# Summing, normalising and scattering tokens inside the expert loop of a mixture-of-experts decoder step

## What is computed

```python
def _moe(x, w_router, router_bias, w_gate, w_up, w_down):
    scores = jax.nn.sigmoid(h @ w_router)
    biased = scores + router_bias
    grp_top = lax.top_k(biased.reshape(T, 4, 4), 2)[0]      # 4 groups of 4 experts
    group = jnp.argmax(grp_top.sum(-1), axis=-1)            # best group
    ...                                                     # top 2 experts inside it
    wts = wts / wts.sum(-1, keepdims=True)
    for e in range(N_EXPERTS):
        he = jax.nn.silu(h @ w_gate[e]) * (h @ w_up[e])
        y = y + gates[:, e:e + 1] * (he @ w_down[e])

x = LN(alpha * x + moe(x))                                  # alpha = 4 ** 0.25
```

## Time and profile before

| | us |
|---|---|
| median of 3 runs (1121.09 to 1126.28) | 1123.17 |
| span of the profiled execution | 1120.2 |
| TensorE busy | 1026.5 (92%) |
| VectorE busy | 497.7 (44%) |
| ScalarE busy | 330.4 (29%) |
| GpSimd busy | 116.9 (10%) |

### The profile page before, as it was taken

The page is one execution under the profiler, slowest core; times in us unless marked ns, Lnnn a source line. Parts: engine busy times, 40 slices in busy tenths (PEclk is TensorE's granted clock), DMA queues, the critical chain, the costliest instruction groups (busy, mean ns, idle before and its releaser), DMA issues.

```text
span 1120.2 us, 25522 instructions
## 1 busy us (share of the span) xinstructions
PE 1026.5 (92%) x10346; PEld 676.0 (60%) x10346; DVE 497.7 (44%) x1257; ACT 330.4 (29%) x877; POOL 116.9 (10%) x140
## 2 busy tenths in 40 slices
PE   9999997599998499999899999989999948999995
PEld 3687454466664267777788887656555535666641
DVE  1581134322222636497636653866623252222217
ACT  0102114133333233223334332165422132333321
POOL 0010000210000300000211110421000011100013
PEclk9999998699999699999999999899999978999998
DMA  9762204999996631122322233394353089999936
GB/s 317 298 88 65 109 38 194 334 351 373 371 402 251 218 151 60 54 86 75 95 75 77 73 115 99 110 388 183 127 222 150 19 324 285 375 372 378 413 105 222
DMA packets 80861, 225.32 MB, mean 201 GB/s; under 512 B 9424, under 2 KB 50432, under 8 KB 62432
## 3 DMA queue, kind: packets, MB, share of 16 engines
q1 hardware_dynamic: 65184, 153.29, 37.7%
q0 software_dynamic: 11968, 57.71, 15.6%
q10 hardware_dynamic: 3584, 12.58, 3.0%
HBM read 201.57 MB, written 40.86 MB: 216 GB/s over the span
## 4 chain that ended last, share of the span: by engine, by line
PE 86%; DMA 5%; DVE 4%; issue 4%; ACT 1%; POOL 0%; DVEq 0%; POOLq 0%; SPq 0%; ACTq 0%
PE bank L1352 16%; PE bank L1256 10%; PE bank L1543 9%; PE bank L1376 8%; PE bank L1451 6%; PE bank L1642 4%; PE bank L1477 3%; PE bank L1334 2%; PE bank L1514 2%; DMA xkept<-x 1%; PE bank L1896 1%; PE bank L1921 1%; PE bank L1267 1%; DMA work<-xkept,idx 1%; PE bank L1855 1%
## 5 line engine op out<-in xcount | busy, mean ns | idle before, releaser
L1256 PE MATMUL bank<-ring,cat 128*128 128x512 f32 x256 | 112.6, 594 | 1.3 <-ACT cat L2088 1.3
L1543 PE MATMUL bank<-xT,ring 128*128 128x288 f32 x448 | 110.9, 407 | 0.0
L1543 PEld LDWEIGHTS bank<-xT,ring 128*128 128x128 f32 x448 | 84.6, 190 | 23.8 <-issue 1.1
L1352 PE MATMUL bank<-ring,work 128*32 128x128 f32 (+1 forms) x1344 | 82.4, 317 | 1.7 <-DVE work L2537 1.7
L1256 PEld LDWEIGHTS bank<-ring,cat 128*128 128x128 f32 x256 | 47.5, 190 | 57.2 <-issue 57.2
L2547 DVE TENSOR_TENSOR work<-work,bank 128x192 f32<-128x192 f32 x32 | 11.3, 354 | 156.3 <-ACT work L2048 156.3
L2556 DVE COPY work<-bank 64x512 f32<-64x512 f32 x64 | 44.0, 688 | 67.2 <-PE bank L1376 66.7
L1352 PEld LDWEIGHTS bank<-ring,work 128*32 128x32 f32 (+1 forms) x1344 | 57.8, 121 | 24.7 <-issue 12.7
L1451 PE MATMUL bank<-xT,ring 128*128 128x288 f32 x256 | 63.1, 407 | 0.0
L2048 ACT ACTIVATE work<-bank 128x192 f32<-128x192 f32 x32 | 10.6, 331 | 162.3 <-PE bank L1352 162.3
L1451 PEld LDWEIGHTS bank<-xT,ring 128*128 128x128 f32 x256 | 48.3, 190 | 13.5 <-issue 0.4
(11 more groups left out here) (459 smaller groups left out, 1893.8 us busy)
## 6 DMA issues: line engine op xcount, KB each, us to landing
ring<-in_stream_dram SPq DMA_DIRECT2D x61, 1024.0 KB, 9.9
work<-in_stream_dram SPq DMA_DIRECT2D x16, 1024.0 KB, 17.1
cat<-in_stream_dram SPq DMA_DIRECT2D x16, 1024.0 KB, 19.1
by_batch<-in_pages_dram SPq DMA_DIRECT2D x128, 128.0 KB, 2.4
x<-in_stream_dram SPq DMA_DIRECT2D x12, 1024.0 KB, 18.3
xT<-in_stream_dram SPq DMA_DIRECT2D x12, 1024.0 KB, 17.3
yrows<-work ACTq DMA_DIRECT2D x32, 384.0 KB, 7.4
lnp<-in_ln_dram POOLq DMA_DIRECT2D x4, 1024.0 KB, 15.2
```

Of the source, the lines that this page charges most:

```text
L1256: i = pe.matmul(bank(n)[0:ROWS[tile], :], cat[:, k, tok(tile)], slot(w[k // 4], 4, 512)[:, k % 4, :], start=(k == 0), stop=(k == KC - 1))
L1352: i = pe.matmul(by_half[rows * q:rows * q + rows, :, to:to + width], xgT[:, e % 2, k, at:at + rows], w[:, :, width * q:width * q + width], ...
L1543: i = pe.matmul(bank(n + s)[:, 0:nn], slot(w, KC, 256)[:, k, P * (m % 2):P * (m % 2) + P], xT[:, k, a:a + nn], start=(k == 0), stop=(k == ...
```

## The change

The gathers of outputs after the loop are gone. Each token is completed in a slot of the later of its two experts:

- The experts are worked in a new order, `ORDER`: 0, 4, 8, 12, 1, 5, ... Position j holds group j % 4, so the two experts of a token are a multiple of four positions apart. The columns of the router follow it, and `route` indexes them so.
- For each slot three things are found in the head of the stage (`weigh_slots` on VectorE, `slot_lists` on TensorE, a copy on ScalarE): the gate divided by alpha, the row of `part_row` if this expert is the token's first, and the row of `final_row` if it is the second. A row number past the end means that the indirect DMA is to leave the slot out (`bounds_check`, `oob_is_err=False`).
- For the expert e - 2, in iteration e: ScalarE copies the wide part of the output; VectorE adds gate times output to the gathered rows (`add_part`). GpSimd scatters the sum of first experts to `parts` in DRAM (`keep_part`, positions 0 to 11), and before the sum of a second expert it fetches these rows over the gathered ones (`fetch_part`, positions 4 to 15). Each of these waits until the scatter of the position before has landed.
- For positions 4 to 15 VectorE averages, centres and applies scale and shift; ScalarE sums the squares; GpSimd takes the power -1/2 (`invert`) and scatters the finished rows (`write_final`) to `xnext` in layer 0 and to the output in layer 1. All 96 slots are computed; only the rows whose second expert this is are written.
- Gathers have six buffers instead of four. GpSimd issues gather(e+3) in iteration e, after fetch_part(e+1) and before keep_part(e-2).
- In layer 0 SP waits for all final scatters and loads the five tiles of x from `xnext`; TensorE then turns them. The ten gathers, the sums by TensorE, the stores by ScalarE and the stores by SP at the end are gone. `parts` is filled once with x from the input by a DRAM to DRAM copy on SP's queue in layer 0's output projection.

Its core:

```diff
+ORDER = [EPG * (j % NG) + j // NG for j in range(N_EXP)]
-NXG = 4
+NXG = 6
+EARLY_ROWS = 4
@@ gpsimd
+                def part_landed(e):
+                    pool.wait_ge(part_kept[layer], 16 * (e + 1))
+
+                def keep_part(e):
+                    if e > 0:
+                        part_landed(e - 1)
+                    elif layer == 0:
+                        pool.wait_ge(parts_cleared, 16)
+                    pool.wait_ge(summed, (N_EXP - 1) * layer + e + 1)
+                    pool.indirect_dma_start(
+                        out=parts, out_offset=bass.IndirectOffsetOnAxis(ap=part_row[0:CAP, e:e + 1], axis=0),
+                        in_=xg[e % NXG][0:CAP, :], in_offset=None,
+                        bounds_check=T - 1, oob_is_err=False).then_inc(part_kept[layer], 16)
+
+                def fetch_part(e):
+                    take(pool, ejob(layer, e, "T1"))
+                    part_landed(e - NG)
+                    if e > NG:
+                        pool.wait_ge(part_back[layer], 16 * (e - NG))
+                    pool.indirect_dma_start(out=xg[e % NXG][0:CAP, :], in_=parts, ... final_row[0:CAP, e:e + 1] ...)
+
+                def invert(e):
+                    pool.wait_ge(squared_rows, final_count(layer, e))
+                    pool.tensor_scalar(row_rstd[...], row_var[...], LN_EPS / ALPHA ** 2, None, ALU.add).then_inc(widened, 1)
+                    pool.wait_ge(widened, final_count(layer, e))
+                    pool.tensor_tensor(row_rstd[...], row_rstd[...], c("minus_half", CAP), ALU.pow).then_inc(inverted_rows, 1)
+
+                def write_final(e):
+                    pool.wait_ge(finished, final_count(layer, e))
+                    if e - NZB >= NG:
+                        pool.wait_ge(rows_final[layer][e % NZB], 16 * ((e - NG) // NZB))
+                    pool.indirect_dma_start(out=xnext if layer < LAYERS - 1 else outs["x"], ... final_row[0:CAP, e:e + 1] ...)
+
+                    for e in range(EARLY_ROWS, NXG):
+                        take(pool, ejob(layer, e - EARLY_ROWS, "T1"))
+                        gather_rows(e)
+                    ln_params(2 * layer + 1)
+                    pool.wait_ge(slots_weighed, layer + 1)
+                    for e in range(2, N_EXP + 2):
+                        if NG <= e + 1 < N_EXP:
+                            fetch_part(e + 1)
+                        if NXG <= e + 3 < N_EXP:
+                            part_landed(e + 3 - NXG)
+                            if e + 3 - NXG >= NG:
+                                pool.wait_ge(finished, final_count(layer, e + 3 - NXG))
+                            gather_rows(e + 3)
+                        if e - 2 < N_EXP - NG:
+                            keep_part(e - 2)
+                        if NG <= e - 2:
+                            invert(e - 2)
+                            write_final(e - 2)
+                    landed_finals(pool, layer)
@@ tensor, ahead of the loop
+                slot_lists()
                 turn_rows(0)
@@ vector, the loop
+                    now(dve.memset(row_sum, 0.0))
+                    weigh_slots(layer)
+                    for e in range(-1, N_EXP):
                         if e + 1 < N_EXP and e != 0:
                             copy_rows(e + 1)
-                        if e < 0:
-                            weigh(layer)
-                        if 0 <= e < N_EXP:
+                        if e >= 2:
+                            add_part(e - 2)
+                        if e - 2 >= NG:
+                            average(e - 2)
+                            center_rows(e - 2)
+                        if e >= 0:
                             n = ejob(layer, e, "GU")
                             ...
+                        if e - 2 >= NG:
+                            affine_rows(e - 2)
+                    add_part(last - 1)
+                    average(last - 1)
+                    add_part(last)
+                    average(last)
+                    for e in (last - 1, last):
+                        center_rows(e)
+                        affine_rows(e)
@@ scalar, the loop, between the copy of the turned result and Silu
+                        if 2 <= e <= N_EXP:
+                            copy_wide(e - 2)
+                        if NG <= e - 2:
+                            square(e - 2)
@@ sync, after the loop
+                        landed_finals(sp, layer)
+                        if layer < LAYERS - 1:
+                            for tile in range(NT):
+                                sp.dma_start(x[0:ROWS[tile], tile, :], xnext[tok(tile), :]).then_inc(tile_loaded[tile], 16)
```

More of the change, by code:

```diff
@@ L82, in constant_table @@
     put("ones", np.ones((P, P)))
-    put("rowbase", np.tile(CAP * np.arange(N_EXP) - 1.0, (P, 1)))
-    put("token", i + P * np.arange(NT)[None, :] * 1.0)
+    put("minus_half", np.full((P, 1), -0.5))
+    put("token", i + P * np.arange(NT)[None, :] - 1.0 * NO_ROW)
     put("lneps", np.full((P, 1), LN_EPS))
@@ L1078, in pool_mixture @@
                     pool.dma_start(xkept[tok(tile), :], x[0:ROWS[tile], tile, :]).then_inc(x_kept, 16)
-                landed(pool, job(f"{layer}.list0"), 1)
+                pool.wait_ge(idx_named, layer + 1)
                 pool.wait_ge(x_kept, 16 * NT * (layer + 1))
-                for e in range(NXG):
+                for e in range(EARLY_ROWS):
                     gather_rows(e)
@@ L2338, in affine @@
                 step(dve.reciprocal(rstd[0:r, one], rstd[0:r, one]))
-                for half, ready in enumerate((ln_left, last)):
+                for half, ready in enumerate((ln_left, ln_done)):
                     cols = slice(512 * half, 512 * half + 512)
```

476 lines of the change are left out of this document (236 added, 240 removed).

## The result

The changed kernel takes 1185.36 us in the median (1178.25 to 1187.5, 4 runs), the kernel before beside it 1124.04. The ratio is 1.053, 95% interval 1.051 to 1.056: slower by 61 us, where 1105.9 and a gain were forecast. The profiled execution spans 1176.4 us, 56.2 more than before. It was the shortest of the four (1176.4 to 1185.6), and between the loops, where no edit of the experiments reaches, the way from the first turned tile of x to the index list of layer 1 takes 539.8 to 546.6 us over all profiles here. So a few us between two spans are no finding; single stretches of the trace are.

What follows compares the result with a forecast made beforehand. It took TensorE to bound the expert loops and aimed at the two tails: 1120.2 - 24.8 - 0.7 + 0.2 + 8.0 = 1102.9, plus 3.0 for the median gives 1105.9 us; range for 8 in 10, 1094 to 1123.

Steps and rivals of the forecast that it cites:

- L: Expert loop: a partial scatter's time to land, taken as 8.1 us from GpSimd's 64-row write of 7.72 plus 0.4.
- GpSimd's chain: Expert loop: scatter landing, then two issues (2.5 us), in series; period 10.6, taken as 10.2 us, costing 8 us in all.
- The prediction's own formula: Loop waiting per layer: nine gathers each lose the period less 9.25, minus 4.6 us in hand; 4.0 us forecast.
- binds hard: Rival for GpSimd's chain in the loops: period 12.0 us, 20 us a layer, 1138 in all; chance 0.13.
- The load falls when TensorE waits: Expert loop: slower TensorE means less traffic and shorter queues, 373 GB/s at 10.3 us; lowered the period to 10.2.
- Traffic: Expert loop: 3,024 rows moved against 3,072 before, skipped slots not counted, so load and queues stay the same.
- The sign of being wrong: Loops: a new wait elsewhere, TensorE behind a blocked VectorE or weights late from grown traffic, would show the prediction wrong.
- The heads: Start of each expert stage: new list work hidden by half a microsecond behind the first gather; +0.2 us for both.
- Layer 1's tail: After the last product: last row ready 9.3 us later, scatter lands in 4.3, end at 1095.4; 24.8 us saved.
- Layer 0's tail: After layer 0's loop: final scatter, reload of x, TensorE turns it at 378.5; 0.7 us saved, within 3 either way.
- VectorE and ScalarE in the loop: Expert loop: some 5.5 of 9.25 us per expert on each, so the edits are free.
- The rule weighed: Loops: GpSimd issues beside two-input VectorE passes could cost 0.25 us more each, period 10.7, 4.5 us more a layer.

Runs made afterwards that it cites:

- e3: The changed kernel with three quarters of each expert weight block from the fourteenth on not loaded; 1122.01 us.
- e2: The changed kernel with all slots of the partial scatter skipped, so it moves no row, while waits and issues stay; 1169.92 us.
- e12: e2 with the partial scatter naming only 8 slots instead of 96, all skipped; 1173.08 us.
- e14: e10 with VectorE's weighing ahead of the branch, without GpSimd's wait for its last scatters, and with weights in 4 KB packets; 1131.3 us, ratio 1.005.
- e16: e14 with the last eighth of each weight block from the fourteenth on not loaded; 1110.16 us.
- e10: The changed kernel with GpSimd's loop waits two experts old: seventh gather buffer, later fetch, two alternating semaphores each for scatters and fetches; 1149.9 us, ratio 1.024.
- e13: The changed kernel with each weight block of the loop loaded by two transfers, in packets of 4 KB instead of 8; 1178.8 us, ratio 1.047.
- e6: The changed kernel with VectorE's weighing of the slots put ahead of the branch; 1175.47 us.

## Why the prediction was wrong

**The step that failed is L, and with it the period of GpSimd's chain.** The mechanism was forecast as it came: fetch and gather follow the landing, and no engine's busy time shows it. Two terms were too small. L was put at 8.1; over the first eight scatters it is 9.4 in the mean in layer 0 and 9.7 in layer 1, 6.7 to 13.4 in single landings. Their median over all 24, 7.6, is under the forecast: the period adds up all landings, and five of those sixteen take 11.7 to 13.4 us. The two issues were put at 2.5; between landing and next start lie 3.43, most of the rest being the 0.84 us ahead of the fetch. The period is 12.8 instead of 10.2 (the first eight distances of layer 0; 13.2 in layer 1). The prediction's own formula, 9 x (12.8 - 9.25) - 4.6, gives 27.4 us a layer, and 31 for layer 1; 26.0 and 29.6 were measured. The rival "binds hard" had the period at 12.0 and was given 0.13.

The 79.5 us between 1105.9 and 1185.36 are then 47.6 in the loops, 12.9 in the heads, 10.7 in layer 1's tail, 2.3 in layer 0's, and 6.0 since the median of the changed kernel lies 9.0 above its profiled span and not 3.0.

**Why I took L too small.** Two steps did it. The nearest row was a single landing of 7.72, and the median of 9.0 under load was kept as a bound only. "The load falls when TensorE waits" lowered 10.6 to 10.2: the weights do land in 9.1 instead of 19.2 us and the engines are at 0.84, but L did not fall with them. The sum behind it doesn't hold for the kernel before either: 3.15 MB and 192 rows in 9.25 us would be 425 GB/s, and the earlier trace rows has 373, for a part of each expert's weights comes out of the 13 blocks that are loaded ahead of the loop and used up in it. L fell far only with three quarters of the weight bytes gone (e3, 3.7 us), while its own rows (e2) and packets (e12) together are worth 1 us. Why it is 8 to 9 us in the serial order even then isn't shown; it may be the gather issued 1.3 us ahead in the same queue, which no run separated.

**Traffic.** The count of bytes was right: 52.87 MB in the loop of layer 0 before and 52.65 after. The packets were not counted: 8808 before and 10933 after. "So the queues stay as full" was wrong in two ways. The engines' work rose from 143 to 148 us with the same bytes (in e14, with more packets, 153). And with 143 of 150 us taken there was hardly room for any more. Once the serial waits are gone this term is worth 8.7 us in layer 0 and 10.3 in layer 1: e14 against e16. The sign of being wrong that the prediction named, weights late because the traffic grew, is what e14 shows.

**The heads** were put at +0.2 us and cost 3.2 and 9.9. The order of steps was right, but the branch was priced at 1 us and is 4.35 in layer 0 and 5.83 in layer 1, there with another 4.08 inside; the matmuls at 2 us and are 3.38. The 8.74 us wait of VectorE in the earlier trace rows was taken as room. A step put behind a branch is paid after the branch, not in the wait that stood there before.

**Layer 1's tail** was right in its steps but for two. The last row is ready at 1162.4, 10.7 us after the last product (9.3 forecast), for the last affine waits 1.84 us for GpSimd's inverse, which was to run beside the centring; the scatter lands within 4 us of its issue (4.3). Then come 9.2 us of GpSimd's end that the prediction lacks, as GpSimd is now the last engine to end. So 14.1 us are saved instead of 24.8; without those 9.2 it would be 23.3. The drain stood in the trace of before, off the path, and was not looked for.

**Layer 0's tail**: 0.7 saved was forecast, 1.6 lost, within the 3 us given. **VectorE and ScalarE in the loop** were free as said: e3 and e16 hold all of their work and keep loops of 149.2 to 150.3. **The rule weighed**: an issue beside the two-input passes costs up to 1.74 instead of 1.00 us (L1138, in the loop of after and at its end), more than the 0.25 that was weighed. It is not what made the period: the fetch and the gather in the chain shown take 1.02 and 0.96.

| part | forecast | measured |
|---|---|---|
| heads | +0.2 | +3.2 and +9.9 |
| loops | +8 | +26.0 and +29.6 |
| tail of layer 0 | -0.7 | +1.6 |
| tail of layer 1 | -24.8 | -14.1 (-23.3 and 9.2 of drain) |

What would make the change pay is not reached: of the 61 us, the order of waits, the weighing ahead of the branch, the missing last wait and the smaller packets give 54 back, and 1131.3 is still 0.5% above the kernel before. Left are some 10 us of DMA work more in layer 0, where 7 were free, and the weights that come late by it in both layers. Keeping layer 0 as it was and changing layer 1 alone might gain a few us: in e14 the way from the first product of layer 1 to the end takes 182.8 us, against 189.2 before. That wasn't tried.

## What to carry to other kernels

When rows are handed over through DRAM inside a loop, count how many transfers old each wait is, not only how many bytes move. Every wait on a transfer of the same iteration puts the whole landing time into the period, and when one is removed the next one has to be looked for. Take the landing time from the mean of many rows under the load that the loop will have, the long ones included, not from one row. Hold the DMA engines' work, share times length, against the loop's length before anything is added, and look how early each block of weights lands ahead of its product. And an engine that becomes the last to do something brings its own branch and its own end onto the path.

## What the runs showed of the hardware

- A partial scatter of 96 slots lands in 3.7 us in the median beside a quarter of the weights, where gathers take 5 (e3). Beside all of the weights in serial order both take some 8, single scatters up to 13.4 (after). With more in flight and 8 KB weight packets they take 12 to 14, single ones up to 22 (e10); with 4 KB packets 8 to 9 in the median again (e14). In the serial order the packet size makes no difference to the mean (e13); why not is open.
- A skipped slot is still a packet: 5296 in GpSimd's queue over the loop of layer 0, with the partial rows moved (after) and without (e2).
- GpSimd's drain at the end takes 7.4 to 9.8 us over the 16 profiles.
- The first instruction of VectorE behind the branch comes 4.4 to 5.8 us late with nothing to wait for in the profile (after), TensorE's 6.0 (e6).
- A TensorE that stands and starts again is slower: in the loop of after its granted clock is 0.93 instead of 0.99, and the same 2072 products take 159.6 busy us instead of 149.3.
